# An encoder layer on one core: projection weight slices 2048 bytes apart, and the first unit's loads and tiles reordered

## The reference

```python
def _encoder_layer(x, w_in, b_if, norm_pre, q_gain, k_gain, w_mo, w_ao, w_out):
    h = _rmsnorm(x, norm_pre)          # x * rsqrt(mean(x*x) + 1e-6) * gain, x is (1536, 1024)
    p = h @ w_in                       # w_in is (1024, 9744)
    q_m, k_m, v_m, o_m, z_m, if_raw, q_a, k_a, v_a, z_a, g_m, g_a = jnp.split(p, idx, axis=-1)
    ...                                # mLSTM both ways on q_m, k_m, v_m with gates if_raw
    ...                                # attention with rotary positions on q_a, k_a, v_a
    merged = jax.nn.sigmoid(g_m) * y_m + jax.nn.sigmoid(g_a) * y_a
    return x + merged @ w_out
```

## Time and profile before

| | us |
|---|---|
| median of 3 runs (2589.54 to 2590.84) | 2590.5 |
| the profiled execution | 2593.84 |
| its span, from the first to the last instruction | 2592.1 |
| PE busy in it | 2417.0 (93%) |
| end of unit 0, begin of unit 1 (PE) | 127.07 |
| last matmul of project begins | 1365.00 |

### The profile page before, as it was taken

One profiled execution on the slowest core, in us unless ns is written; L12 is line 12 of the kernel. 1 busy time (PEld: TensorE's weight loads), 2 busy tenths in 40 slices (PEclk: granted clock), 3 DMA queues, 4 the chain that ended last, 5 costly groups with the idle time before them and its releaser, 6 DMA issues. The chain is left out here.

```text
span 2592.1 us, 32337 instructions
## 1 busy us (share of the span) xinstructions
PE 2417.0 (93%) x12053; PEld 2005.8 (77%) x12053; DVE 993.1 (38%) x1819; ACT 916.1 (35%) x1719; POOL 796.0 (31%) x564
## 2 busy tenths in 40 slices
PE   4899999999999999999996999898959995999998
PEld 4878888888888888888885777777748884888887
DVE  2310022222222212110115888887858883113222
ACT  3311111111112221210005888777747873211121
POOL 2021122222222222221104777676710002533320
PEclk9999999999999999999998999999989997999999
DMA  3122233333333333322225222222044433743332
GB/s 135 63 80 90 90 102 107 123 108 119 102 123 123 123 119 123 123 88 97 96 98 173 88 86 88 86 86 85 13 147 139 151 127 130 252 167 129 118 138 82
DMA packets 167782, 292.65 MB, mean 113 GB/s; under 512 B 9840, under 2 KB 73168, under 8 KB 167632
## 3 DMA queue, kind: packets, MB, share of 16 engines
q1 hardware_dynamic: 147184, 230.41, 27.9%
q10 hardware_dynamic: 20448, 60.31, 5.8%
HBM read 183.53 MB, written 107.15 MB: 112 GB/s over the span
## 5 line engine op out<-in xcount | busy, mean ns | idle before, releaser
L460 POOL TENSOR_TENSOR a_w_lo<-a_raw,a_w_hi 128x512 fp32r<-128x512 f32 (+1 forms) x152 | 199.2, 1313 | 892.4 <-DVE a_w_hi L555 883.7
L798 PE MATMUL a_acc<-a_w_hi,a_act_hi 128*128 128x512 f32 (+1 forms) x960 | 362.5, 378 | 22.9 <-DVE a_act_lo L549 19.8
L798 PE MATMUL a_acc<-a_act_hi,a_w_hi 128*128 128x512 f32 x960 | 382.3, 398 | 0.0
L800 PE MATMUL a_acc<-a_act_hi,a_w_lo 128*128 128x512 f32 x960 | 378.3, 394 | 0.0
L799 PE MATMUL a_acc<-a_act_lo,a_w_hi 128*128 128x512 f32 x960 | 376.2, 392 | 0.0
L800 PE MATMUL a_acc<-a_w_hi,a_act_lo 128*128 128x512 f32 (+1 forms) x960 | 359.1, 374 | 0.0
L799 PE MATMUL a_acc<-a_w_lo,a_act_hi 128*128 128x512 f32 (+1 forms) x960 | 359.1, 374 | 0.0
L555 DVE CAST a_w_hi<-a_raw 128x512 fp32r<-128x512 f32 x144 | 61.2, 426 | 760.0 <-PE a_acc L800 749.0
L1545 POOL TENSOR_TENSOR t_prob<-t_prob,t_rsum 128x1024 f32<-128x1024 f32 (+1 forms) x192 | 308.2, 1609 | 126.4 <-DVE t_rsum L1565 126.4
L745 ACT ACTIVATE a_stage<-a_acc 128x512 f32<-128x512 f32 x216 | 125.0, 602 | 481.6 <-PE a_acc L800 473.3
L798 PEld LDWEIGHTS a_acc<-a_w_hi,a_act_hi 128*128 128x128 f32 x960 | 182.1, 190 | 59.3 <-POOL a_w_lo L460 12.1
(11 more groups left out here) (208 smaller groups left out, 3990.2 us busy)
## 6 DMA issues: line engine op xcount, KB each, us to landing
a_raw<-w_in SPq DMA_DIRECT2D x72, 512.0 KB, 3.9
p_feat<-a_stage ACTq DMA_DIRECT2D x40, 768.0 KB, 3.8
p_tok<-a_stage ACTq DMA_DIRECT2D x36, 768.0 KB, 4.3
stacks<-a_flat SPq DMA_DIRECT2D x72, 256.0 KB, 2.5
t_q<-stacks SPq DMA_DIRECT2D x8, 1536.0 KB, 6.7
t_k<-stacks SPq DMA_DIRECT2D x16, 768.0 KB, 9.2
m_raw<-p_feat SPq DMA_DIRECT2D x24, 512.0 KB, 4.0
f_stage<-p_feat SPq DMA_DIRECT2D x12, 1024.0 KB, 7.2
```

The source lines that it names most:

```text
L460: nc.gpsimd.tensor_sub(w_lo[cut], raw_of(u, k), w_hi[cut].bitcast(F32)).then_inc(lo_made, 1)
L798: nc.tensor.matmul(out, stat_hi, mov_hi, start=first, stop=False)
L800: return nc.tensor.matmul(out, stat_lo, mov_hi, start=False, stop=last)
```

## The change

1. `w_hi` and `w_lo` become flat tiles of 9 times 512 columns. Units 1 to 18 use slices of 512 columns, 2048 bytes apart, and `w_lo` begins 18432 bytes (9 times 2048) behind `w_hi`. Unit 0 keeps slices of 528 columns in the same room. `await_slice` follows: the slices of unit 1 now lie over those of unit 0 and wait for the matmuls of the last token tile, slice by slice (a new `slice_free` in unit 0).
2. All four pairs of raw slices of unit 0 are loaded without a wait: two into `raw`, two into `stage`, which is empty then. Odd low parts are made on DVE, even ones on POOL.
3. The transposes of tile t, with act high and act low, come before the first unit of tile t - 1. Some due times around them move.
4. ACT's table for Sqrt is loaded by a small activation at the start.
5. The slices of unit 1 are due 0.2 tick earlier, and with that k = 7 (17.05) comes before "offsets" (17.1) on DVE.

```diff
     for t in range(TT):
-        at("sp", t - (8.0 if t < 3 else 3.9), "load x", t)
+        at("sp", (-9.0, -8.0, -6.0)[t] if t < 3 else t - 3.9, "load x", t)
         at("act", t - 2.9, "square", t)
-        at("dve", t - 2.7, "mean", t)
-        at("act", t - 2.6, "root", t)
+        at("dve", t - 2.8, "mean", t)
+        at("act", t - 2.7, "root", t)
         at("dve", t - 2.5, "norm", t)
-        at("pe", t - 0.6, "transpose", t)
-        at("act", t - 0.55, "act high", t)
-        at("dve", t - 0.5, "act low", t)
+        at("pe", t - 1.05, "transpose", t)
+        at("act", t - 1.0, "act high", t)
+        at("dve", t - 0.9, "act low", t)
         at("pe", t, "first unit", t)
         at("act", t + 1.1, "first out", t)
     for k in range(KT):
         if k % 2 == 0:
-            at("sp", (-7.9, -6.9, -2.8, -2.7)[k // 2], "load weights", 0, k)
-        at("act", (-3.0, -3.0, -2.2, -2.2, -1.7, -1.7, -1.6, -1.6)[k] + 0.01 * k, "first high", k)
-        at("pool", -2.5 + 0.1 * k, "low", 0, k)
+            at("sp", -8.5 + 0.8 * (k // 2), "load first weights", k)
+        at("act", (-2.8, -2.8, -2.6, -2.6, -1.95, -1.95, -1.65, -1.65)[k] + 0.01 * k, "first high", k)
+        at("dve" if k % 2 else "pool", (-2.75, -2.7, -2.55, -2.4, -2.0, -1.9, -1.6, -1.55)[k], "first low", k)
     for u in range(1, len(projection_units())):
         start = SPAN * u
         for k in range(KT):
-            ready = start - (5.9 if u > 1 else 0.0) + STEP * k if k else start - 6.2
+            ready = start - (5.9 if u > 1 else 0.2) + STEP * k
             if k % 2 == 0:
-                at("sp", ready - (2.2 if u > 1 or k else 2.0), "load weights", u, k)
+                at("sp", ready - (2.2 if u > 1 else 1.4), "load weights", u, k)
...
-        w_hi = sc.sb("w_hi", [P, SLICES, NIF + WCOL], F32R)
-        w_lo = sc.sb("w_lo", [P, SLICES, NIF + WCOL], F32R)
-        raw = sc.sb("raw", [P, 2, 2, NIF + WCOL])
+        w_hi = sc.sb("w_hi", [P, SLICES * WCOL], F32R)
+        w_lo = sc.sb("w_lo", [P, SLICES * WCOL], F32R)
+        raw = sc.sb("raw", [P, 2, 2 * (NIF + WCOL)])
...
-        def ring(u, k):
-            return (KT * u + k) % SLICES
+        def slice_at(u, k):
+
+            if u == 0:
+                return slice(k * (NIF + WCOL), (k + 1) * (NIF + WCOL))
+            i = (KT * (u - 1) + k) % SLICES
+            return slice(i * WCOL, (i + 1) * WCOL)
 
         def await_slice(eng, u, k):
 
-            was = KT * u + k - SLICES
-            if was >= 0:
-                v, j = was // KT, was % KT
-                if v == 0 or j == KT - 1:
-                    eng.wait_ge(acc_full, CREDIT + groups_before(v + 1))
-                else:
-                    eng.wait_ge(slice_free, CREDIT + (KT - 1) * (v - 1) + j + 1)
+            v, j = divmod(KT * (u - 1) + k - SLICES, KT)
+            v = v + 1
+            if v < 1:
+                v, j = 0, min(k, KT - 1) if u == 1 else KT - 1
+            if j == KT - 1:
+                eng.wait_ge(acc_full, CREDIT + groups_before(v + 1))
+            else:
+                eng.wait_ge(slice_free, CREDIT + (KT - 1) * v + j + 1)
...
+                    elif kind == "load first weights":
+                        k = n[0]
+                        src = w_cols[:, k:k + 2, C_IF:C_IF + NIF + WCOL]
+                        if k < KT // 2:
+                            sp.dma_start(raw[:, k // 2, :].rearrange("p (k c) -> p k c", k=2), src)\
+                                .then_inc(raw_loaded[k // 2], 16)
+                        else:
+                            room = stage[:].rearrange("p a b c -> p (a b c)")
+                            at_col = (k - KT // 2) * (NIF + WCOL)
+                            sp.dma_start(room[:, at_col:at_col + 2 * (NIF + WCOL)].rearrange("p (k c) -> p k c", k=2), src)\
+                                .then_inc(first_loaded[k // 2 - 2], 16)
...
+                    elif kind == "first low":
+                        k = n[0]
+                        dve.wait_ge(first_hi, CREDIT + k + 1)
+                        cut = (slice(None), slice_at(0, k))
+                        nc.vector.tensor_sub(w_lo[cut], first_raw_of(k), w_hi[cut].bitcast(F32)).then_inc(first_lo, 1)
...
+                act.wait_ge(zeroed, CREDIT + 5)
+                nc.scalar.activation(stat[:, 0, 2:3], ones[:, 0:1], ACT.Sqrt)
...
                                 last = three(acc[b][:, 0:cut.stop - cut.start], act_hi[:, k, s], act_lo[:, k, s],
-                                             w_hi[:, k, cut], w_lo[:, k, cut], k == 0, k == KT - 1)
+                                             w_hi[:, w], w_lo[:, w], k == 0, k == KT - 1)
+                                if t == TT - 1 and part and k < KT - 1:
+                                    last.then_inc(slice_free, 1)
```

More of the change, by code:

```diff
@@ L329, in quarters_before @@
             return 4 * (u - NU_P + 2)
[L331 to L335, removed]
         nc.all_engine_barrier()
@@ L454, in _ @@
                         u, k = n
[L455 to L459, removed]
-                        nc.gpsimd.tensor_sub(w_lo[cut], raw_of(u, k), w_hi[cut].bitcast(F32)).then_inc(lo_made, 1)
+                        pool.wait_ge(hi_made, CREDIT + KT * (u - 1) + k + 1)
+                        cut = (slice(None), slice_at(u, k))
+                        nc.gpsimd.tensor_sub(w_lo[cut], raw_of(u, k), w_hi[cut].bitcast(F32)).then_inc(lo_made, 1)
+                    elif kind == "first low":
+                        k = n[0]
+                        pool.wait_ge(first_hi, CREDIT + k + 1)
+                        cut = (slice(None), slice_at(0, k))
+                        nc.gpsimd.tensor_sub(w_lo[cut], first_raw_of(k), w_hi[cut].bitcast(F32)).then_inc(lo_made, 1)
                     elif kind == "swap gains":
@@ L552, in _ @@
                         u, k = n
-                        dve.wait_ge(raw_loaded[(KT * u + k) // 2 % 2], CREDIT + raw_count(u, k))
+                        dve.wait_ge(raw_loaded[pair_of(u, k) % 2], CREDIT + 16 * (pair_of(u, k) // 2 + 2))
                         await_slice(dve, u, k)
-                        nc.vector.tensor_copy(w_hi[:, ring(u, k), 0:WCOL], raw_of(u, k)).then_inc(hi_made, 1)
+                        nc.vector.tensor_copy(w_hi[:, slice_at(u, k)], raw_of(u, k)).then_inc(hi_made, 1)
+                    elif kind == "first low":
+                        k = n[0]
+                        dve.wait_ge(first_hi, CREDIT + k + 1)
+                        cut = (slice(None), slice_at(0, k))
+                        nc.vector.tensor_sub(w_lo[cut], first_raw_of(k), w_hi[cut].bitcast(F32)).then_inc(first_lo, 1)
                     elif kind == "gate product":
@@ L719, in _ @@
                         k = n[0]
-                        act.wait_ge(raw_loaded[k // 2 % 2], CREDIT + raw_count(0, k))
-                        nc.scalar.activation(w_hi[:, k, :], raw_of(0, k), ACT.Copy).then_inc(first_hi, 1)
+                        if k < KT // 2:
+                            act.wait_ge(raw_loaded[k // 2], CREDIT + 16)
+                        else:
+                            act.wait_ge(first_loaded[k // 2 - 2], CREDIT + 16)
+                        nc.scalar.activation(w_hi[:, slice_at(0, k)], first_raw_of(k), ACT.Copy).then_inc(first_hi, 1)
                     elif kind == "first out":
@@ L822, in _ @@
                                 if t == 0 and part == 0:
-                                    pe.wait_ge(lo_made, CREDIT + k + 1)
+                                    if k % 2:
+                                        pe.wait_ge(first_lo, CREDIT + k // 2 + 1)
+                                    else:
+                                        pe.wait_ge(lo_made, CREDIT + k // 2 + 1)
                                 if part == 0 and k % 4 == 0:
                                     pe.wait_ge(act_lo_made[k // 4], CREDIT + t + 1)
+                                base = slice_at(0, k).start
+                                w = slice(base + cut.start, base + cut.stop)
                                 last = three(acc[b][:, 0:cut.stop - cut.start], act_hi[:, k, s], act_lo[:, k, s],
-                                             w_hi[:, k, cut], w_lo[:, k, cut], k == 0, k == KT - 1)
+                                             w_hi[:, w], w_lo[:, w], k == 0, k == KT - 1)
+                                if t == TT - 1 and part and k < KT - 1:
+                                    last.then_inc(slice_free, 1)
                             last.then_inc(acc_full, 1)
@@ L830, in _ @@
                         u, half, k = n
-                        i = ring(u, k)
+                        w = slice_at(u, k)
                         if half == 0:
-                            pe.wait_ge(lo_made, CREDIT + KT * u + k + 1)
+                            pe.wait_ge(lo_made, CREDIT + lo_count(u, k))
                         for b in range(NB):
@@ L839, in _ @@
                                 last = three(acc[b][:], act_hi[:, k, s], act_lo[:, k, s],
```

(6 more changed lines are left out.)

24 lines of the change are left out of this document (19 added, 5 removed).

## The result

The changed kernel takes 2545.0 us (2543.9 to 2545.9, 4 runs) against 2590.7 (4 runs); ratio 0.9822, interval 0.9805 to 0.9840. That is 45.7 us less. The forecast was 2546.5, range 2540 to 2562. The profiled execution took 2544.44 with a span of 2542.6, so 49.4 less than the profiled one of before.

A forecast was written before the change was run, and what follows sets the result against it. PE, busy 2417 of 2592 us, was taken to bound the kernel. Terms 21.7, 14.0, 1.9 and 6.0 sum to 43.6 us: profiled 2593.84 becomes 2550.2, 3.3 less for the median gives 2546.9, put as 2546.5; range 2540 to 2562.

The forecast's parts named there:

- pace of units 1 to 18: Units 1 to 18: slices laid out as in finish run at finish's 226.7 ns a matmul, saving 21.7 us.
- tiles one step ahead: Unit 0: transposes run before the previous tile's first unit, so PE hardly waits for act low; saves 14.0 us.
- start, up to the end of first unit 0: Kernel start: first unit 0 begins 1.1 us earlier and less of it runs at low clock (0.8); together 1.9 us.
- unit 1's wait and clock: Unit 1: PE's 3.1 us wait and the half clock after it go, saving 6.0 us.
- term of 2.2 us for 72 interruptions: Units 1 to 18: rope transposes interrupt the projection 72 times, 0.03 us each, taken off the pace gain of 23.9.
- (a): Rival on pace: addresses don't matter, finish is faster through long runs on one PSUM bank; 21.9 saved, 2568.6 us; chance 0.13.
- (b): Rival on pace: slices reach only the projection's best step, 4.12 us; 10.5 instead of 21.7 us, time 2558; chance 0.10.
- (c): Rival on pace: slices of one phase collide in memory in each matmul; at 238 ns the time is 2603; chance 0.03.
- (d): Rival in units 0 and 1: a new wait replaces the old ones, giving back 8 of 20 us; 2554.5; chance 0.06.
- its blocked and its unblocked case: Start: whether DVE's low parts and norms wait for POOL; first unit 0 begins 0 to 2.7 us earlier, 1.1 taken.

## Why the prediction was right, step by step

| part | forecast, us | in the profiled executions, us |
|---|---|---|
| pace of units 1 to 18 | 21.7 | 22.9 |
| tiles one step ahead | 14.0 | 15.3 |
| start, up to the end of first unit 0 | 1.9 | 3.0 |
| unit 1's wait and clock | 6.0 | 6.0 |
| sum in project | 43.6 | 47.2 |

The right column comes from starts of PE rows, of one profiled execution each. The pace is what the old spacing costs behind the beginning of unit 1: in that kernel 1341.77 - 109.80, in the changed one 1317.82 - 108.77. The tiles: 127.07 - 38.94 before, 108.77 - 35.91 after. The start: first unit 0 ended at 38.94 and now at 35.91. Unit 1 is the rest of (1365.00 - 127.07) - (1317.82 - 108.77) = 28.9.

**The pace** was right in cause and place: finish's layout, carried over, gave finish's pace to the hundredth. The prediction's guess that a run behind transposes needs some matmuls until it is fast was right too, but its term of 2.2 us for 72 interruptions was over-sized: of the 23.9 without any, 22.9 came. Rivals (a) and (b) asked for steps of 4.16 or 4.12; those of units 16 and 17 are all 4.08. Rival (c) fell with them, and (d) too, since no new wait came. What the prediction had only half: it named multiples of 2048, and 256 is what is needed, in each of the tensors. The Trainium skill's rule that TensorE waits on nobody ("SBUF — State Buffer", section "Who interferes with whom") doesn't describe this: two kernels with the same instructions and 64 bytes between two tiles differ by 1.5 us in 65.3 in each token unit. The measurement decides. Through which port, or by what, the time is lost isn't shown.

**The tiles**: a group of 8 transposes costs 0.79 us to the next product, not 0.95; ten groups make 1.6 us. The first units take 5.91 instead of 5.87, 0.4 the other way.

**The start** was put at 29.5 for first unit 0; it was 29.17. The mechanism, DVE waiting for POOL, was the right one. Taking the low parts off DVE gave 3.8 us, where the prediction had 2.7 between its blocked and its unblocked case, with their work still on DVE. The low clock then took 1.6 us less, not 0.8: first unit 0 takes 35.91 - 29.17 = 6.74 us instead of 8.38. Up to 1 us of this is luck: it hangs on when the clock rises, and in other kernels with the same unit 0 unit 1 begins up to 1.0 us later.

**Unit 1**: 6.0 as forecast; the term was read from rows of the old kernel itself. As a price for such a wait it doesn't carry over: brought back alone it costs 4.4, since PE waits 2.3 us and not 3.1 and the clock is down for 3.4 us and not 6.8.

The parts came to 3.6 us more than forecast in project and to 2.3 more behind it. Trace against trace the forecast was therefore 5.8 us short, 43.6 for 49.4. Between the medians only 45.7 remain, as said above, and 43.6 meets 45.7. That the number came out within 2 us is in part luck: the terms were 3.6 us too small and 2.3 us came from stages without a term, and the distance of the two profiled executions from their medians hides most of it. And 2546.9, what the sum gives, was put down as 2546.5; that is no rounding, and it brought the forecast 0.4 us nearer to 2545.0.

## What to carry to other kernels

Where TensorE is busy without gaps, read its pace from the starts of matmuls of one form, by stage and by ring slot: a few nanoseconds between two stages are a find, here 23 us. Lay out ring slots and the tiles behind them so that every operand begins at a multiple of 256 bytes, and check it for each tensor, since a small tile between two large ones is enough to lose it; don't expect it to help where transposes come in after every eight matmuls or fewer. And before work is given to VectorE to help GpSimd, look in the trace whether its subtraction runs beside GpSimd's or waits for it: here the help cost 3.4 us.

## What the runs showed that I had not expected

In a long run without transposes, fp32r matmuls of 512 columns start 226.7 ns apart at 2.4 GHz, which is 544 cycles, 32 more than columns. It is no rule for other widths: at 272 columns it would give 126.7 ns, and 125.3 were measured. Off the multiple of 256 the mean was 230.8 to 232.5 ns, whatever the offset: 64 bytes in one tensor (66.82 us a unit), 64 bytes more from slice to slice (66.81), 128 bytes (66.70). So it looks like the loss of a rhythm more than a price by the byte. And after a wait of 3.1 us the clock stayed at 0.50 (1.2 GHz) for 6.8 us in one kernel, after one of 2.3 us for 3.4 us in another, so the same kind of wait had two prices.
